# Storing each expert's 64 result rows as two transfers, one for each half of the columns

## What is computed

```python
g_idx = jnp.argmax(g_logits, axis=-1)                  # one group of 4
top_v, top_i = lax.top_k(e_logits, TOP_K_IN_GROUP)     # two of its 8 experts
wts = g_prob[:, None] * jax.nn.softmax(top_v, axis=-1)
...
def expert_block(args):
    tok_b, e = args
    xb = xpad[tok_b]
    h = jax.nn.silu(xb @ w_gate[e]) * (xb @ w_up[e])
    return h @ w_down[e]
...
y = jnp.zeros((t + 1, d), out.dtype).at[buf_tok].add(out)[:t]
```

## Time and profile before

| what | us |
|---|---|
| median of 3 runs | 1737.29 (1737.02 to 1742.86) |
| the profiled execution | 1738.25 |
| its span, from first to last instruction | 1736.1 |
| TensorE busy with matmuls | 1482.2 (85%) |
| VectorE busy | 706.7 (41%) |
| ScalarE busy | 488.0 (28%) |
| GpSimd busy | 38.1 (2%) |
| transfers on SP's and ScalarE's queue | 304.69 MB, 44.5% of 16 engines' time |
| mean granted clock of TensorE | 0.92 |

### The profile page before, as it was taken

The page is one execution under the profiler, slowest core; times in us unless marked ns, Lnnn a source line. Parts: engine busy times, 40 slices in busy tenths (PEclk is TensorE's granted clock), DMA queues, the critical chain, the costliest instruction groups (busy, mean ns, idle before and its releaser), DMA issues.

```text
span 1736.1 us, 17979 instructions
## 1 busy us (share of the span) xinstructions
PE 1482.2 (85%) x6858; PEld 1014.6 (58%) x6858; DVE 706.7 (41%) x1297; ACT 488.0 (28%) x723; POOL 38.1 (2%) x73
## 2 busy tenths in 40 slices
PE   6999979977777777788663699998899999999976
PEld 5787766433333323233221588877788888888865
DVE  4676655101010101010002575644526666666645
ACT  5543440100000000000001522232434444444532
POOL 1010000000000000000002001000000000000000
PEclk9998998988888979889876699998999999999988
DMA  8746444978887885477784555422122121212101
GB/s 354 284 143 226 170 162 178 380 321 338 342 325 308 324 337 207 192 309 309 307 327 188 223 201 202 148 88 75 49 97 92 54 98 49 97 58 89 49 1 61
DMA packets 35791, 336.88 MB, mean 194 GB/s; under 512 B 3540, under 2 KB 3668, under 8 KB 17364
## 3 DMA queue, kind: packets, MB, share of 16 engines
q1 hardware_dynamic: 28612, 304.69, 44.5%
q0 software_dynamic: 6624, 29.89, 4.9%
q10 hardware_dynamic: 432, 0.60, 0.1%
HBM read 312.62 MB, written 22.54 MB: 193 GB/s over the span
## 4 chain that ended last, share of the span: by engine, by line
PE 45%; DMA 5%; DVE 2%; ACT 2%; issue 2%; SPq 1%; POOL 0%; DVEq 0%; ACTq 0%; POOLq 0%
PE ps L290 44%; DMA spare<-in_wts_dram 2%; DMA ring<-in_wts_dram 1%; PE ps L718 1%; DMA y_scratch<-gate 1%; SPq L2062 1%; ACT ar L860 0%; DVE b_NL L1293 0%; DVE ar L1285 0%; DMA ar<-y_scratch,rt 0%; DVE hres L1776 0%; ACT b_NH L869 0%; PE ps L296 0%; DVE ar L1959 0%; ACT ar L1073 0%
## 5 line engine op out<-in xcount | busy, mean ns | idle before, releaser
L290 PE MATMUL ps<-ring,ar 128*64 128x512 f32 x800 | 271.1, 662 | 49.4 <-issue 37.3
L290 PE MATMUL ps<-ar 128*64 128x512 f32 (+5 forms) x798 | 247.8, 504 | 43.0 <-issue 14.0
L290 PE MATMUL ps<-b_NH,b_WH 128*128 128x512 f32 x704 | 187.0, 401 | 8.2 <-DVE b_NL L1293 4.5
L290 PE MATMUL ps<-b_NH,b_WL 128*128 128x512 f32 x704 | 181.3, 393 | 0.0
L290 PEld LDWEIGHTS ps<-ring,ar 128*64 128x64 f32 x800 | 84.5, 152 | 165.0 <-issue 163.5
L290 PEld LDWEIGHTS ps<-ar 128*64 128x64 f32 (+3 forms) x798 | 101.0, 168 | 134.6 <-issue 121.6
L290 PE MATMUL ps<-spare,ar 128*64 128x512 f32 x416 | 143.5, 662 | 36.2 <-issue 35.8
L1226 DVE TENSOR_TENSOR b_WL<-ring,b_WH 128x1024 fp32r<-128x1024 f32 x112 | 136.6, 1220 | 92.7 <-ACT b_WH L812 92.7
L290 PE MATMUL ps<-b_NL,b_WH 128*128 128x512 f32 x704 | 173.7, 389 | 0.0
L1654 DVE TENSOR_TENSOR ar<-ar,ps 128x256 f32<-128x256 f32 x34 | 14.3, 421 | 371.7 <-ACT ar L1003 369.7
L812 ACT ACTIVATE b_WH<-ring 128x1024 fp32r<-128x1024 f32 x112 | 118.1, 1055 | 160.1 <-PE ps L290 158.3
(11 more groups left out here) (269 smaller groups left out, 1887.1 us busy)
## 6 DMA issues: line engine op xcount, KB each, us to landing
ring<-in_wts_dram SPq DMA_DIRECT2D x84, 2048.0 KB, 16.5
ar<-in_wts_dram SPq DMA_DIRECT2D x24, 2048.0 KB, 21.7
spare<-in_wts_dram SPq DMA_DIRECT2D x24, 2048.0 KB, 22.3
ring<-in_wmod_dram SPq DMA_DIRECT2D x24, 512.0 KB, 4.8
ar<-in_wmod_dram POOLq DMA_DIRECT2D x24, 512.0 KB, 4.2
y_scratch<-gate POOLq DMA_DIRECT2D x11, 1024.0 KB, 21.4
y_scratch<-gate SPq DMA_DIRECT2D x22, 256.0 KB
y_scratch<-ar SPq DMA_DIRECT2D x12, 256.0 KB
```

The lines of the kernel that those rows point to most:

```text
L290: return pe.matmul(o, l, m, start=start, stop=stop, skip_group_check=True)
```

## The change

`store` issues two transfers in place of one. Before, the target was seen as 2 halves of the columns x 64 tokens x 512 values, with the halves outermost, and the source was the whole buffer of 128 partitions. Now the first transfer writes columns 0 to 511 of the 64 rows from partitions 0 to 63, the second columns 512 to 1023 from partitions 64 to 127. Each adds 16 to the store's semaphore, so every wait on `y0`, `y1`, `y2` and `ty` counts in 32s, and the count that ScalarE adds in place of a store is 32. The bytes and the contiguous runs of 512 values are the same.

```diff
--- before.py
+++ after.py
@@ -1010,7 +1010,7 @@
 
                 act.wait_ge(S["m_d2"], n + 1)
                 if n >= 3:
-                    act.wait_ge(S[f"y{n % 3}"], 16 * (n // 3))
+                    act.wait_ge(S[f"y{n % 3}"], 32 * (n // 3))
                 elif n == 0:
                     act.wait_ge(S["ovx"], 1)
                 act.activation(ysb[n % 3], ps[:, 5, :], ACT.Copy).then_inc(S["m_y"], 1)
@@ -1042,10 +1042,10 @@
                     if n:
                         for v in ("t_xg", "t_sg", "t_ht", "t_y"):
                             act.wait_ge(S[v], n)
-                        act.wait_ge(S["ty"], 16 * n)
+                        act.wait_ge(S["ty"], 32 * n)
                     for v in ("t_xg", "t_sg", "t_ht", "t_y"):
                         act.sem_inc(S[v], 1)
-                    act.sem_inc(S["ty"], 16)
+                    act.sem_inc(S["ty"], 32)
                 if n:
                     result(n - 1)
                 if n % 4 == 0 and n + 4 < NE:
@@ -1712,7 +1712,7 @@
                 dve.wait_ge(S["t_tx"], u + 1)
                 if u:
                     dve.wait_ge(S["t_up"], u)
-                    dve.wait_ge(S["ty"], 16 * u)
+                    dve.wait_ge(S["ty"], 32 * u)
                 dve.tensor_tensor(xT3.rearrange("p (h j) s -> p h j s", h=2),
                                   ps[:, 6, :].rearrange("p (j h s) -> p h j s", j=4, h=2),
                                   bc(cols[:, C_G2:C_G2 + 8].rearrange("p (h j o) -> p h j o", h=2, o=1), 128, 2, 4, 64),
@@ -2022,13 +2022,13 @@
             n_over, third = read_ctl(pool)
             for j in range(NOV):
                 with pool.If(n_over > j):
-                    pool.wait_ge(S["ty"], 16 * (NE + j + 1))
+                    pool.wait_ge(S["ty"], 32 * (NE + j + 1))
             pool.wait_ge(S["ovx"], 1)
             pool.wait_ge(S["m_d2"], NE)
             pool.wait_ge(S["m_y"], NE)
             for j in range(3):
-                pool.wait_ge(S[f"y{j}"], 16 * len(range(j, NE, 3)))
-            pool.wait_ge(S["ty"], 16 * NE)
+                pool.wait_ge(S[f"y{j}"], 32 * len(range(j, NE, 3)))
+            pool.wait_ge(S["ty"], 32 * NE)
             pool.wait_ge(S["yzero"], 16 * 11)
             for m in range(8):
                 p, c = m // 2, m % 2
@@ -2089,7 +2089,9 @@
 
             def store(b, y, sem):
 
-                sp.dma_start(y_d[b * CAP:(b + 1) * CAP, :].rearrange("t (q c) -> q t c", q=2), y).then_inc(S[sem], 16)
+                for q in range(2):
+                    sp.dma_start(y_d[b * CAP:(b + 1) * CAP, 512 * q:512 * q + 512],
+                                 y[64 * q:64 * q + 64, :]).then_inc(S[sem], 16)
 
             for n in range(NE):
                 for m in range(3):
@@ -2123,14 +2125,14 @@
                     expert(0, 2).then_inc(S["v_w0"], 16)
                     sp.wait_ge(S["t_y"], NE + j + 1)
                     store(2 * NE + j, ysb3, "ty")
-                    sp.wait_ge(S["ty"], 16 * (NE + j + 1))
+                    sp.wait_ge(S["ty"], 32 * (NE + j + 1))
 
             sp.wait_ge(S["m_d2"], NE)
             sp.wait_ge(S["m_y"], NE)
             sp.wait_ge(S["m_hh"], NE)
             for j in range(3):
-                sp.wait_ge(S[f"y{j}"], 16 * len(range(j, NE, 3)))
-            sp.wait_ge(S["ty"], 16 * NE)
+                sp.wait_ge(S[f"y{j}"], 32 * len(range(j, NE, 3)))
+            sp.wait_ge(S["ty"], 32 * NE)
             sp.dma_start(fgr, row(R_FG, 1024)).then_inc(S["fgain"], 16)
             sp.wait_ge(s_yg[7], 16)
             for i in range(P_C0 + 1, P_DIL + 3):
```

## The result

The changed kernel takes 1614.24 us (median of four runs, 1612.94 to 1616.23) against 1739.78 us before, a ratio of 0.928 (95% interval 0.926 to 0.930). Two later comparisons with the same kernel gave 1619.11 and 1616.03 us, ratios 0.931 (0.929 to 0.933) and 0.929 (0.928 to 0.931). The forecast was 1599 us with a range of 1588 to 1630: the direction and the mechanism hold, and the time lies 15 us above the forecast. Of the forecast gain of 138.1 us the medians show 125.5.

A forecast was written before the change was run, and what follows sets the result against it. The bound was taken to be the two DMA engines carrying their share of panels plus all stores; steps of 72.3, 19.4, 36.0 and 10.4 us sum to 138.1, taking 1737.3 to 1599 us, range 1588 to 1630.

The forecast's parts named there:

- The bound and the spread: Expert stage: two DMA engines carry all stores, 5.14 us per expert; halves of 64 rows use 16 engines, 0.64 us.
- The period: Time per expert where the DMA engines bound: 14.73 us of panels plus 0.64 of store, 15.37 in place of 19.87 us.
- Step 1: Stretch up to the up of expert 19: panels allow it at 557.3 in place of 629.62, 72.3 us gained.
- the 2 us "for the way in and out": Term added to panel and store times when working out when expert 5's up can start: 2 us.
- Its sign for expert 5: Up of expert 5: its panels are ready at 342.1, TensorE is there at 347.8, so it no longer waits.
- Step 2: Experts 19 and 20 with a third block, 629.62 to 744.79: shorter waits for stores and less lower clock, 19.4 us gained.
- Step 3: Stretch from 744.79 to the up of expert 31 at 911.51: its panels allow it at 875.5, 36.0 us gained.
- Step 4: The end, behind the up of expert 31: the last store lands in 3.3 us in place of 13.74, 10.4 us gained.
- the cover of SP's issues: SP's second store issue costs nothing, as the engines have queued panels; without that cover 34 x 0.5 = 17 us.
- A: New period not reached: 8 engines or small rows, 0.65 us per period (1612); plus TensorE's lower clock, 1631; chance 0.17.
- B: No change, 1737 us: store stays on two engines or halves serialise; a skill rule prefers one transfer; chance 0.05.
- C: Slower: halves stay on two engines and SP's second issue lies on the path, 20 us more, 1757 us; chance 0.02.

## Why the prediction was right, point by point, and where it was short

**The bound and the spread.** Right: two DMA engines carried all stores. Shown by the kernel with 62 + 2 rows (as slow as before), by the one with 32 + 32 rows (as fast as the changed one) and by the full share after. That 64 rows go over 16 engines was argued from the panels and is shown by the windows at 1.01 and by the 0.6 us that a further store costs.

**The period.** Forecast 15.37, measured 15.53 as a mean. Five of twelve hit the forecast within 0.1 us; four are 0.7 to 1.3 us late with the engines full all the same (453.15 and 499.79 above), and shorter ones make up a part of it. In 12 periods 2 us are left. The rate held: over these 186.3 us the engines moved 426 GB/s, 79.4 MB, where twelve experts have 78.6 MB, and the 0.8 MB more are these 2 us; which transfers they are is open.

**Step 1**, 4.6 us short: 12 periods at 0.16 are 1.9 us. The rest is the start: the ready time of expert 7 was to be 342.1 + 2 x 15.37 = 372.8, its up began at 375.56, 2.8 us later, though TensorE was free at 373.7. So the start lies 2.8 us behind the sum; the 2 us "for the way in and out" are the term that no row had shown for this place. Its sign for expert 5 came true: that up no longer waits (348.11, with no idle ahead of it).

**Step 2**, 1.3 us short: VectorE's wait for a store is gone as forecast (621.48 above; TensorE waits 0.78 us for it); the other wait shrank to 6.20 us, not to 13.49 - 9.1 = 4.4. It ended 20.6 us behind the issue of the first panel of that group (638.29), where 18.8 were worked out.

**Step 3**, 1.6 us short: the last three periods took (791.24 - 743.82) / 3 = 15.81 us.

**Step 4** right: 2.91 us for the last store's landing, forecast 2.8 and 0.5.

**What failed** is the sentence that all that follows the gathers only starts earlier. The last store's landing had hidden other work, the loading of TensorE's instructions past twelve blocks that aren't taken. The prediction named the cover of SP's issues, but not what the 13.74 us of landing covered on the other engines. The loading itself became slower too, since the gathers now fall into it. Behind the last store 8.2 us were given back, half of the 16.1 us that are missing between the two profiled executions: 5.5 us by this loading, 2.7 us with no cause shown. Without the loading the medians came down by 8.3 and 8.8 us.

**The rivals.** A's first half, less gain by a longer period, is what steps 1 and 3 show, but at 0.16 us in step 1 and 0.44 us in the last three periods of step 3, not 0.65, and not because of fewer engines: the store costs its 0.6 us. Its second half, the lower clock in the gaps, occurred and cost nothing: the up of expert 7 took 8.78 us behind 1.86 us of idle, the window at 499.79 has a granted clock of 0.83, and the panels are later all the same. In one period, 453.15 to 469.34 at a granted clock of 0.89, TensorE was busy for all of its 16.19 us and was the bound; the next one took 14.37 us and made that up. B and C are out: the rule that rival B names supposes that the one transfer uses all engines, which this one did not, and SP's further issues cost nothing even when doubled.

## What to carry to other kernels

A stretch in which the DMA share stands near 2/16 while the issuing engine is blocked in an issue was here a transfer that used too few engines; look at the outermost dimension of either side, and count the fullest engine's bytes, since all later transfers of the queue wait for it. Cut it so that the rows outermost divide evenly over 16 engines, as 64 and 32 rows did here and 62 + 2 or 34 + 30 did not, even at the price of more transfers.

When a wait on the path goes, list what each other engine did under it, its instruction loading too, and ask which transfers will now fall together. Here conditional blocks that are never taken cost time to pass, and one condition around all of them made that go away.

## What was not expected of the hardware

- SP is held up by the fullest DMA engine even in short transfers: with 62 and 2 rows SP was blocked for up to 18.45 us in the issue of four stores of 256 KB together, where before it had been blocked in the next panel (15.89 us).
- The granted clock did not follow the length of the idle time alone. Behind 1.86 and 2.46 us of idle (375.56 and 422.57 in the changed kernel) the up fell to the lower level on its way: 8.78 us for its 32 matmuls in place of 7.09, and a granted clock of 0.80 in the window 422.57 to 431.16, though its first matmul still took 0.61 us. Behind 1.70 us (407.29) and, in the kernel before, 2.98 us (431.18) the windows 407.29 to 422.57 and 431.18 to 438.30 have 1.00. So the first matmul alone does not tell the level of an up.
- Seven pages of instructions took TensorE from 808.07, the end of its last expert, to 843.53, when gathers and panels kept the DMA engines at 0.76 to 1.00 of their time from 813 on. Before, the same seven pages had started by 949.9, 21.9 us behind the end of its last expert.
